# First FFN w2 tile waits per hidden K tile, and C tile products stand before the B transposes in the SSD convolution

## The reference

```
def swiglu(h, w1, w3, w2):                     # both layers; hidden width 2816 = 22 tiles of 128
    return (silu(h @ w1) * (h @ w3)) @ w2

proj = concatenate([hc, hx]) @ w_in            # SSD mixer
z, xbc, dt_raw = split(proj, [INNER, INNER + CONV_DIM])
xbc = silu(depthwise_conv5(xbc) + conv_b)      # context and latent apart
xs, bm, cm = split(xbc, [INNER, INNER + GROUPS * STATE])
```

## Time and profile before

| | |
|---|---|
| median of 3 runs | 1246.41 us (1242.51 to 1246.70) |
| profiled execution, its own time | 1245.67 us |
| its span, first to last instruction | 1243.9 us |
| granted TensorE clock, mean | 0.977 of 2.4 GHz |
| PE busy | 1162.7 us, 93% |
| DVE busy | 879.7 us, 71% |
| ACT busy | 591.6 us, 48% |
| POOL busy | 223.3 us, 18% |
| DMA | 168.23 MB, mean 135 GB/s |

### The profile page before, as it was taken

One profiled execution on the slowest core, in us unless ns is written; L12 is line 12 of the kernel. 1 busy time (PEld: TensorE's weight loads), 2 busy tenths in 40 slices (PEclk: granted clock), 3 DMA queues, 4 the chain that ended last, 5 costly groups with the idle time before them and its releaser, 6 DMA issues.

```text
span 1243.9 us, 19284 instructions
## 1 busy us (share of the span) xinstructions
PE 1162.7 (93%) x6954; PEld 974.1 (78%) x6954; DVE 879.7 (71%) x1311; ACT 591.6 (48%) x984; POOL 223.3 (18%) x166
## 2 busy tenths in 40 slices
PE   5799999898999999999999889999999897999997
PEld 3577776678988888878888778887677797999996
DVE  0896888975887777774665688888999666555453
ACT  3647888733532323232222556446466445666442
POOL 0201444422100000000111100005877211000010
PEclk9899999999999999989999999999999898999999
DMA  9543222240575555554552142221221343655562
GB/s 380 190 129 126 61 93 86 69 170 1 189 240 171 186 194 202 178 187 142 161 162 68 58 122 81 86 84 50 70 68 55 116 153 115 192 180 189 150 186 71
DMA packets 48176, 168.23 MB, mean 135 GB/s; under 512 B 5233, under 2 KB 6513, under 8 KB 47857
## 3 DMA queue, kind: packets, MB, share of 16 engines
q1 hardware_dynamic: 48112, 167.38, 40.4%
HBM read 166.31 MB, written 1.05 MB: 135 GB/s over the span
## 4 chain that ended last, share of the span: by engine, by line
PE 69%; DVE 17%; ACT 7%; issue 4%; DMA 1%; SPq 1%; POOL 1%; DVEq 0%; ACTq 0%
PE bank L1666 20%; PE bank L1668 20%; PE bank L1667 20%; DVE scratch L1442 5%; DVE w_lo L1073 3%; PE bank L2091 2%; ACT w_hi L607 2%; DMA raw<-in_w_in 1%; ACT scratch L912 1%; PE bank L2103 1%; DVE softmax_max L1244 1%; PE bank L2124 1%; ACT conv_in L909 1%; PE bank L2113 1%; DVE mla_h_lo L1264 1%
## 5 line engine op out<-in xcount | busy, mean ns | idle before, releaser
L1073 DVE TENSOR_TENSOR w_lo<-raw,w_hi 128x1024 fp32r<-128x1024 f32 (+1 forms) x226 | 281.4, 1247 | 158.7 <-ACT w_hi L607 158.5
L607 ACT ACTIVATE w_hi<-raw 128x1024 fp32r<-128x1024 f32 (+1 forms) x226 | 230.8, 1023 | 274.0 <-PE bank L1668 252.0
L1666 PE MATMUL bank<-ffn_h_lo,w_hi 128*128 128x256 f32 (+1 forms) x736 | 246.0, 334 | 8.9 <-DVE ffn_h_lo L1110 5.6
L1667 PE MATMUL bank<-ffn_h_hi,w_hi 128*128 128x256 f32 (+1 forms) x736 | 245.3, 333 | 0.0
L1668 PE MATMUL bank<-ffn_h_hi,w_lo 128*128 128x256 f32 (+1 forms) x736 | 245.2, 333 | 0.0
L1666 PEld LDWEIGHTS bank<-ffn_h_lo,w_hi 128*128 128x128 f32 x736 | 140.4, 191 | 24.3 <-issue 6.0
L1668 PEld LDWEIGHTS bank<-ffn_h_hi,w_lo 128*128 128x128 f32 x736 | 140.4, 191 | 14.6
L1667 PEld LDWEIGHTS bank<-ffn_h_hi,w_hi 128*128 128x128 f32 x736 | 140.5, 191 | 14.4
L462 POOL TENSOR_TENSOR scratch<-scratch 128x512 f32<-128x512 f32 (+1 forms) x24 | 34.6, 1443 | 618.8 <-ACT scratch L616 618.8
L1666 PE MATMUL bank<-ffn_hidden_lo,w_hi 128*128 128x256 f32 (+1 forms) x374 | 125.0, 334 | 5.8 <-DVE ffn_hidden_lo L1402 5.8
L1666 PE MATMUL bank<-ssd_h_lo,w_hi 128*128 128x256 f32 (+2 forms) x360 | 125.3, 348 | 5.0 <-DVE ssd_h_lo L1347 2.3
(11 more groups left out here) (264 smaller groups left out, 2147.0 us busy)
## 6 DMA issues: line engine op xcount, KB each, us to landing
raw<-in_w SPq DMA_DIRECT2D x120, 512.0 KB, 4.3
scratch<-in_vec_w SPq DMA_DIRECT2D x56, 512.0 KB, 3.6
vec_weights<-in_vec_w SPq DMA_DIRECT2D x24, 512.0 KB, 3.6
raw<-in_w_xbc SPq DMA_DIRECT2D x24, 512.0 KB, 3.5
ada_start<-in_ada_w SPq DMA_DIRECT2D x8, 1024.0 KB, 17.2
raw<-in_w_z SPq DMA_DIRECT2D x16, 512.0 KB, 3.5
raw<-in_w_so SPq DMA_DIRECT2D x16, 512.0 KB, 3.6
raw<-in_w SPq DMA_DIRECT2D x16, 384.0 KB, 3.8
```

Source lines behind the costliest of these rows:

```text
L607: A(wh[s % RING][:, 0:c], raw[s % RING][:, 0:c], ACT.Copy).then_inc(w_hi, 1)
L1073: V.tensor_tensor(wl[s % RING][:, 0:c], raw[s % RING][:, 0:c], wh[s % RING][:, 0:c].bitcast(f32), SUB).then_inc(w_lo, 1)
L1666: mm(o, lh, rl, start=first, stop=False)
L1667: mm(o, lh, rh, start=False, stop=False)
```

## The change

For output tile m = 0 of each FFN the wait for all hidden tiles goes, and `tile` waits for the low part of each hidden tile ahead of that K tile's three products. For m >= 1 nothing waits for the hidden tiles. In the SSD the C tile t = 4 to 7 now stands ahead of the transposes of B tile t - 4, and the C tiles wait for 1, 2, 5 and 6 copies out of the banks. On DVE the low parts of weight blocks n+4 for t = 0 and 1 move ahead of that tile's taps. ACT, POOL and SP have the same lists as before.

```diff
@@ DVE, conv
+                if not late(t, 2):
+                    lo(n + 4, s + 4)
                 dve.wait_ge(conv_init, t + 1)
                 for r in range(1, 5):
...
-                lo(n + 4, s + 4)
+                if late(t, 2):
+                    lo(n + 4, s + 4)
@@ PE, tile
-            def tile(n, s, o, h, l, k0, nk, first, final):
+            def tile(n, s, o, h, l, k0, nk, first, final, hidden=None):
 
                 pe.wait_ge(w_lo, n + 1)
                 for k in range(nk):
+                    if hidden is not None:
+                        pe.wait_ge(hid_lo, hidden + k0 + k + 1)
@@ PE, w2
-            def w2(q0, m, n, nt, h, l):
+            def w2(q0, m, n, nt, h, l, hidden):
 
                 pe.wait_ge(added, q0 + m - 1)
                 for r, (k0, nk) in enumerate(((0, 8), (8, 8), (16, KH - 16))):
-                    tile(n + r, n + r, bank[m % 2][:, 0:nt], h, l, k0, nk, r == 0, r == 2).then_inc(w_used, 1)
-
-            pe.wait_ge(hid_lo, KH)
+                    tile(n + r, n + r, bank[m % 2][:, 0:nt], h, l, k0, nk, r == 0, r == 2,
+                         hidden if m == 0 else None).then_inc(w_used, 1)
+
             for m in range(7):
-                w2(ADD1, m, g0(m), TOK, lambda k: U0h[:, k, :], lambda k: U0l[:, k, :])
+                w2(ADD1, m, g0(m), TOK, lambda k: U0h[:, k, :], lambda k: U0l[:, k, :], 0)
@@ PE, the convolution
             def conv_tile(t, n, s, u, kind):
-                if late(t, 2):
+                if late(t, 8):
                     pe.wait_ge(conv_up, t - 1)
+                else:
+                    pe.wait_ge(conv_up, (1, 2, 5, 6)[t - 4])
...
             four_halves(4, BC, (bank[0], bank[1], bank[4], bank[5]), H1h, H1l)
-            to_tokens(0, 0, 0)
-            to_tokens(1, 1, 1)
             for t in range(4, 8):
                 conv_tile(t, BC + t, BC + t, t % 2, "C")
-                if t < 6:
-                    to_tokens(t - 2, t % 2, t - 2)
+                to_tokens(t - 4, t % 2, t - 4)
@@ PE, second FFN
-            pe.wait_ge(hid_lo, 2 * KH)
             for m in range(8):
-                w2(ADD3, m, G1 + 3 * m, LAT, lambda k: U1h[:, k, :], lambda k: U1l[:, k, :])
+                w2(ADD3, m, G1 + 3 * m, LAT, lambda k: U1h[:, k, :], lambda k: U1l[:, k, :], KH)
```

## The result

| | before | after |
|---|---|---|
| median, 20 runs each | 1245.93 us (1241.88 to 1248.45) | 1249.35 us (1247.60 to 1251.15) |
| profiled execution, its own time | 1245.67 us | 1248.18 us |
| its span | 1243.9 us | 1246.4 us |
| granted TensorE clock, mean | 0.977 | 0.974 |
| PE busy | 1162.7 us | 1160.4 us |

The ratio is 1.0028, 95% interval 1.0019 to 1.0037: 3.5 us slower (2.4 to 4.6 by the interval), so a real loss, but within the 0.5% that was called no change, and inside the range. The forecast was +0.9 us on the profiled execution, where +2.5 were measured.

The account below looks back on a forecast made before the run. PE, busy 93% of the span, was taken to bound the kernel. -5.85 and -4.56 us for the FFNs and +11.3 for the convolution gave +0.9 on 1245.67, so 1246.6; stated 1247.0, range 1241 to 1253.

Parts of the forecast that it names:

- The FFN steps: Turns from hidden tiles to w2: without the wait and low clock, -5.85 us in the first FFN, -4.56 in the second.
- the ring would feed w2: Both FFNs: weight block four, first used 66 products on, arrives in time, so w2 is not starved; costed at nothing.
- The lower bound of 6.1: Both FFNs' least gain if the clock falls anyway: 3.2 us in the first, 2.9 in the second.
- (A): The forecast itself: convolution loses 8.5 to 12.8 us, FFNs gain 8.9 to 10.4, total 1244 to 1250.5; chance 0.77.
- The low parts: Convolution, DVE: low parts ahead of taps 0 and 1 cost 2.1 us each, chain 4.2 us late from tile 1 on.
- The order: Convolution: transposes 2 and 3 queue behind C tiles 6 and 7, which wait for copies 4 and 5; with low parts, +11.3 us.
- the tiles' clock: C tiles 6 and 7 on PE: partly at low clock behind idle time, 4.6 and 4.1 us against 2.94 at full clock.
- The bound of 12.8: Convolution's loss in us if C tiles 6 and 7 both run wholly at half clock.
- its first paragraph: What bounds the kernel: PE, 93% of the span busy; idle PE time before a full stretch costs its own length.
- (B): Slower rival, convolution: PE stays at 1.2 GHz through the dt product, +7.0 us, 1252.7 or 1253.4; chance 0.10.
- (C): Faster rival, convolution: waiting for transposes 2 and 3 costs nothing, only the low parts' 4.2 us stay, 1240.2; chance 0.07.
- (D): Rival, FFNs: w2 is starved by the ring or the wait stays; 1257.7 if all gain goes, 1252.5 if half; chance 0.06.

Follow-up runs that it names:

- ffn_only: The kernel before with only the change's FFN part, the convolution as before: 1236.28 us, ratio 0.9910 to before.
- low_only2: The kernel before with only DVE's low parts of blocks n+4 moved ahead of the taps for t = 0 and 1: ratio 1.0034 to before.
- spare_banks2: The change with low parts unmoved, transposes t-4 ahead of C tile t, C tiles 6 and 7 in banks 6 and 7: 1231.16 us, 0.9887 to before.
- transposes_first: The change, but with transposes 2 and 3 ahead of C tiles 6 and 7: ratio 0.9969 to before.
- change_spare: The change, but C tiles 6 and 7 go to banks 6 and 7 and wait for no copy: ratio 0.9950 to before.
- filled2: The change with extra unread products on idle PE, 24 ahead of C tile 6 and 7 ahead of C tile 7: ratio 1.0084 to before.

## Why the prediction was right

**The FFN steps** (-5.85, -4.56) stand: at the turns themselves -5.87 (9.37 to 3.50) and -4.53 (7.96 to 3.43), and -10.5 to -11.2 in the time of ffn_only. That the -5.91 at copy 0 lies as near is partly luck, as ffn_only has -4.42 there. That the ring would feed w2 without the pause stands too: no idle time in 8.7 and 7.6 us behind the turns. The 22 added waits cost nothing that can be seen: the first 66 products of w2 take 15.4 us, 0.233 each. The lower bound of 6.1, that the clock falls anyway, is refuted by the windows of both turns in the change. The 8.9 that (A) gives as the FFNs' least has no working behind it.

**The low parts** (+4.2) stand: copies 1 and 2 are 2.08 and 4.17 us later behind copy 0 than before, and low_only2 has +4.15 and +4.2.

**The order** stands step by step, and what failed is the size of one term, the tiles' clock:

| | forecast | trace after |
|---|---|---|
| idle time before tile 6, tile 7 | 11 and 3.4 us | 11.25 and 3.46 us |
| tile 6 to its transposes | 4.6 | 4.85 |
| copy 5 late, against copy 0 | 9.4 | 9.62 |
| tile 7 to its transposes | 4.1 | 5.29 |
| copy 6 (behind taps 5) late | 14.15 | 15.69 |
| copy 8 late | 11.3 | 12.71 |

I gave tile 7 the low clock for half its length, since the idle time before it was short. But behind PE's idle time of 3.46 us the clock stood at 0.50 over the whole tile. That is 1.2 of the 1.4 us by which the stage was undersized, and most of the 1.6 between +0.9 and +2.5. The bound of 12.8, both tiles wholly at half clock, was the truer value.

The rest, from the profiled pair's +2.5 to the measured +3.5, stays open; +2.5 lies within the interval of 2.4 to 4.6. Single executions of before lie 6.6 us apart, those of after 3.6. Only one execution of each kernel has a trace, so that the spread can't be traced to its stretches.

One part of the account is luck. The sum is the difference of two large terms, -10.4 and +11.3, and the miss in the second, an eighth of it, is larger than the sum of +0.9. That the total still fell inside the range owes something to the range being 12 us wide.

**What its first paragraph missed.** It counts PE's idle time at its length and takes PE to be full in the x stage. In the B/C stage of before PE stood for 4.54 us in front of transposes 1,

```profile
716.30 0.80 PE L2021 MATMUL bank<-tab,scratch 128*128 128x128 f32 x4 [4.54 <-ACT scratch L924]
```

and ran in part at the low clock behind it (0.69 in the mean of 716.3 to 721.8). Neither delayed the chain: copies 1 to 4 stand 5.60 us apart all the same. And the x stage gives nothing back, as was said, but because its chain sets its length (spare_banks2), not because PE is full in it.

**The rivals.** (A) held. (B), the low clock through the dt product, did not come: 1.00 from 741.2 on, with PE at work without a pause from 735.37. The pattern that was cited there from the Trainium skill ("TensorE: Matmul & The Clock Gate", section "HAM oscillation — how this bites in real kernels": short groups of matmuls between waits each start at the low clock) did hold for tiles 6 and 7, behind 11.25 and 3.46 us of idle time. It did not for C tile 5, which ran at 1.00 behind 2.28 us, and it ended with the first long stretch of work. (C), nothing lost by the transposes' place, is refuted by transposes_first: 6.7 us of the stage are that. (D) is refuted by ffn_only.

## What to carry to other kernels

A wait for everything is worth cutting into waits for each piece when the consumer's own work is longer than the last producer's tail; its price is the pause and the low clock behind it, here 6.3 and 4.1 us for two turns. Before an instruction is moved ahead of another one in a hand-written order, follow what it waits for: C tiles ahead of the transposes cost nothing where they waited for no bank (change_spare), and 8.6 us where the bank's release stood behind work that needed those transposes' neighbours (6.7 for their place, tile 7's low clock among them, and the rest for tile 6's low clock). And when two parts of a change are of opposite sign, time them apart: -11 and +12 looked like nothing.

## What was not expected of the hardware

- A product of two plain fp32 operands with 512 columns took 0.84 us at full clock and left two records (24 products and 48 records in 20.2 us, filled2), where a product of the rounded halves of the same shape takes 0.2346. I had read the price of one record, 0.43, as that of the product.
- The longer idle time did not cost more clock: tile 7, behind 3.46 us, took 2.3 us more than the 2.95 at full clock, tile 6, behind 11.25 us, 1.9 more. I had expected the opposite order.
- Idle times of 2.28 and 0.5 us in front of C tile 5 and transposes 1 after the change left the clock at full level: the tile took 2.9 us. But the length of one idle time does not settle it: in spare_banks2 C tile 6 stands behind idle times of 1.71 and 1.97 us with a tile of work between them, starts at full clock, and from 716.8 to 720.2 has 0.51.
